# Long convolution woven between weight units in a two-layer diffusion block, and slabs of modulation weights moved

## What is computed

```python
def centred_long_conv(z, h):
    zf = jnp.fft.rfft(z.astype(jnp.float32), n=n_fft, axis=1)
    hf = jnp.fft.rfft(h, n=n_fft, axis=0)
    y = jnp.fft.irfft(zf * hf[None], n=n_fft, axis=1)[:, n_tok // 2:n_tok // 2 + n_tok]
def hyena_mixer(h, w_in, b_in, conv_w, conv_b, filt, skip, w_out, b_out):
    u = centred_short_conv(h @ w_in + b_in, conv_w, conv_b)
    x1, x2, v = jnp.split(u, HYENA_ORDER + 1, axis=-1)
    z = x1 * (centred_long_conv(v, filt[:, 0]) + v * skip[0])
    z = x2 * (centred_long_conv(z, filt[:, 1]) + z * skip[1])
    return z @ w_out + b_out
...
        x = x + g1 * y_lat
        x = x + g2 * sq_relu_mlp(modulate(rms_norm(x, norm_mlp_g[i]), sh2, sc2), mlp_w1[i], mlp_w2[i])
```

## Time and profile before

| | |
|---|---|
| median of 3 runs | 2640.75 us (2637.38 to 2641.97) |
| the profiled execution's own time | 2644.23 us |
| its span | 2642.4 us |
| TensorE busy | 2471.6 us (94%) |
| VectorE busy | 1955.2 us (74%) |
| ScalarE busy | 1167.6 us (44%) |
| mean granted TensorE clock | 0.964 |
| DMA | 610.10 MB, mean 231 GB/s |

### The profile page before, as it was taken

One profiled execution on the slowest core, in us unless ns is written; L12 is line 12 of the kernel. 1 busy time (PEld: TensorE's weight loads), 2 busy tenths in 40 slices (PEclk: granted clock), 3 DMA queues, 4 the chain that ended last, 5 costly groups with the idle time before them and its releaser, 6 DMA issues.

```text
span 2642.4 us, 40626 instructions
## 1 busy us (share of the span) xinstructions
PE 2471.6 (94%) x13316; PEld 2077.0 (79%) x13316; DVE 1955.2 (74%) x2322; ACT 1167.6 (44%) x1595; POOL 0.2 (0%) x4
## 2 busy tenths in 40 slices
PE   6879989798999999999989899899899999999998
PEld 2248867587888888888878778787788888888887
DVE  6767777687987878878878888888765565565665
ACT  2334256435344444444454325234544444444444
POOL 0000000000000000000000000000000000000000
PEclk9989998898999999999989999999899999999998
DMA  8857865576988888888777658576665565665653
GB/s 306 319 183 247 277 194 171 168 269 234 351 299 279 281 279 280 269 283 280 263 241 243 211 195 278 173 247 213 201 190 187 187 190 186 187 190 185 189 189 121
DMA packets 441193, 610.10 MB, mean 231 GB/s; under 512 B 18875, under 2 KB 383644, under 8 KB 439068
## 3 DMA queue, kind: packets, MB, share of 16 engines
q1 hardware_dynamic: 439676, 599.98, 68.4%
q10 hardware_dynamic: 1440, 9.18, 1.0%
HBM read 596.50 MB, written 10.49 MB: 230 GB/s over the span
## 4 chain that ended last, share of the span: by engine, by line
PE 71%; DVE 13%; issue 6%; ACT 6%; DMA 3%; SPq 0%; DVEq 0%; ACTq 0%
PE ps L359 42%; PE ps L368 22%; DVE acc L456 2%; DVE w_lo L444 2%; PE ps L1100 2%; ACT w_hi L440 2%; DMA raw<-in_mlp_w 1%; ACT hm L875 1%; DVE sm L1751 1%; DMA raw<-in_attn_w_out 1%; PE ps L1136 1%; PE ps L1117 1%; DVE u L646 1%; PE ps L1326 1%; ACT probs L1465 1%
## 5 line engine op out<-in xcount | busy, mean ns | idle before, releaser
L444 DVE TENSOR_TENSOR w_lo<-raw,w_hi 128x1024 fp32r<-128x1024 f32 x720 | 877.3, 1224 | 495.5 <-ACT w_hi L440 491.7
L440 ACT ACTIVATE w_hi<-raw 128x1024 fp32r<-128x1024 f32 x720 | 758.9, 1059 | 1030.5 <-PE ps L368 813.6
L359 PE MATMUL ps<-lat,w_hi 128*128 128x512 f32 x3136 | 816.2, 400 | 31.0 <-DVE lat L864 18.3
L359 PEld LDWEIGHTS ps<-lat,w_hi 128*128 128x128 f32 x3136 | 575.9, 192 | 140.1 <-issue 24.5
L359 PE MATMUL ps<-alt,w_hi 128*128 128x512 f32 x2624 | 674.4, 396 | 11.2 <-DVE alt L1738 5.9
L359 PEld LDWEIGHTS ps<-alt,w_hi 128*128 128x128 f32 x2624 | 476.3, 190 | 97.9 <-issue 6.7
L368 PEld LDWEIGHTS ps<-lat,w_lo 128*128 128x128 f32 x3136 | 435.3, 192 | 31.4 <-DVE w_lo L444 0.4
L368 PE MATMUL ps<-lat,w_lo 128*128 128x256 f32 x3136 | 447.6, 284 | 0.0
L456 DVE SCALAR_TENSOR_TENSOR acc<-slab,silu,acc 128x1024 f32<-128x1024 f32 x300 | 380.2, 1280 | 8.9 <-DMA slab<-in_mod_w 6.8
L368 PEld LDWEIGHTS ps<-alt,w_lo 128*128 128x128 f32 x2624 | 363.7, 192 | 26.4 <-DVE w_lo L444 0.6
L368 PE MATMUL ps<-alt,w_lo 128*128 128x256 f32 x2624 | 374.4, 283 | 0.2 <-DVE w_lo L444 0.2
(11 more groups left out here) (191 smaller groups left out, 1512.4 us busy)
## 6 DMA issues: line engine op xcount, KB each, us to landing
raw<-in_mlp_w SPq DMA_DIRECT2D x512, 512.0 KB, 3.7
slab<-in_mod_w SPq DMA_DIRECT2D x352, 512.0 KB, 5.9
raw<-in_hy_w_in SPq DMA_DIRECT2D x96, 512.0 KB, 6.6
raw<-in_attn_w_in SPq DMA_DIRECT2D x48, 512.0 KB, 4.6
raw<-in_mod_w SPq DMA_DIRECT2D x32, 512.0 KB, 6.7
raw<-in_attn_w_out SPq DMA_DIRECT2D x32, 512.0 KB, 4.9
raw<-in_hy_w_out SPq DMA_DIRECT2D x32, 512.0 KB, 7.0
spec_dram<-spec ACTq DMA_DIRECT2D x8, 1024.0 KB, 6.9
```

What stands on the lines that cost most here:

```text
L359: e.matmul(ps[:, bank, :], w_hi[:, n % RING, kk, fb * P:(fb + 1) * P], t[:, kb, :], start=(kb == 0), stop=False)
L440: e.activation(w_hi[:, n % RING], raw[:, n % RING], ACT.Copy).then_inc(hi_ready, 1)
L444: e.tensor_tensor(w_lo[:, n % RING], raw[:, n % RING], w_hi[:, n % RING].bitcast(F32), ALU.subtract).then_inc(split_ready, 1)
```

## The change

The chunk loop is unrolled in all engines, and each step of the long convolution is given a place by number: t counts units from the chunk's first, 24 to a chunk, and steps with t of 24 or more stand between units of the next chunk. For the last chunk they stand in the first call of the output projection, whose units take another order so that the ones that need the last chunk's z come last, and whose readout (`FirstOut`) starts behind the seventh unit. PSUM banks 4 to 7 serve the convolution, u of v becomes double-buffered (u0), and skip is part of multiply. The hyena keeps eight slabs a chunk, in two of its three calls (halves 8 and 9, both closed by one `pe_close`); half 7 comes with the output projection, halves 10 and 11 with the second MLP's first four up calls, eight slabs a call, finished behind them.

```diff
-        SL_HOUT = Slabs(1, [11], 4, M_HOUT)
+            return Slabs(1, [8 + c // 2], 4, M_HY + 2 * c, 8 * (c % 2), c // 2)
+        HOUT_ORDER = ((0, 0), (0, 1), (0, 2), (1, 0), (1, 1), (1, 2), (0, 3), (1, 3))
+        SL_HOUT = Slabs(1, [7], 4, M_HOUT)
+        SL_UP1 = Slabs(1, [10, 11], 8, M_UP1)
+        def at_conv(places, c, k, n):
+            for (t, hf), what in places.items():
+                for chunk in (c - 1, c):
+                    if 0 <= chunk < 4 and t == 24 * (c - chunk) + 8 * k + n:
+                        yield what, chunk, hf
...
+            for c in range(4):
+                    sp_iter(e, T_HY + 3 * c + k, a["hy_w_in"], 0, (c + part * 4) * 512, k, sl_hy(c) if k < 2 else None,
+                            {(0, 4): 2 * c - 1, (1, 1): 0 if c == 0 else None, (2, 1): 2 * c if c else None}, k)
...
+            CONV_PE = {(14, 0): "turn0", (15, 1): "turn0", (18, 0): "spectrum0", (19, 1): "spectrum0",
+                       (23, 0): "invert0", (24, 1): "invert0", (28, 0): "turn1", (29, 1): "turn1",
+                       (32, 0): "spectrum1", (33, 1): "spectrum1", (37, 0): "invert1", (38, 1): "invert1"}
...
-                pe_finish(e, M_HY + 4 * c + 4, FIN_HY + c, 1)
+            for n in range(8):
+                g, j = HOUT_ORDER[n]
+                if n == 0:
+                    invert(3, 0, 1)
+                if n in (2, 3):
+                    turn(3, 1, n - 2)
+                if n in (4, 5):
+                    spectrum(3, 1, n - 4)
+                if n == 6:
+                    invert(3, 1, 0)
+                    invert(3, 1, 1)
+                    pe_close(e, M_HOUT, FIN_HY, 7)
+                pe_unit(e, T_HOUT, n, g, j, alt, (z_ready, 8 if j == 3 else 6))
...
+            CONV_ACT = {(17, 0): "copy0", (18, 1): "copy0", (31, 0): "copy1", (32, 1): "copy1", (42, 0): "round", (43, 1): "round"}
...
+            CONV_DVE = {(13, 0): "fold0", (13, 1): "fold0", (21, 0): "multiply0", (22, 1): "multiply0",
+                        (26, 0): "combine0", (27, 1): "combine0", (35, 0): "multiply1", (36, 1): "multiply1",
+                        (40, 0): "combine1", (41, 1): "combine1", (43, 0): "rest", (44, 1): "rest"}
...
+            for n in range(8):
+                dve_split(e, T_HOUT, n)
+                if n in (1, 2):
+                    combine(3, 0, n - 1)
+                    fold(3, 1, n - 1)
+                if n in (4, 5):
+                    multiply(3, 1, n - 4)
+                if n == 6:
+                    combine(3, 1, 0)
+                    combine(3, 1, 1)
+                    round_rest(3, 0)
+                    round_rest(3, 1)
+                    dve_close(e, FIN_HY, [mod_col(1, 8), mod_col(1, 9)], 7)
+            dve_slabs(e, SL_HOUT, 0, 0, 4)
+            first_h.dve_head(e, T_HOUT, 0)
...
             def gains_mlp1():
-                e.wait_ge(mod_ready, FIN_HOUT + 1)
+                dve_finish(e, FIN_HOUT, [mod_col(1, 7)])
...
-            mlp(1, 0, None, None, None, None, None)
+            mlp(1, 0, None, SL_UP1, None, None, (FIN_UP1, [mod_col(1, 10), mod_col(1, 11)]))
```

More of the change, by code:

```diff
@@ L1374, in _, with turn @@
-            pe_call(e, T_HOUT, 4, alt, lambda i: lambda j: (z_ready, 8), 4)
-            pe_enter(e, 4, 9, lambda: pe_finish(e, M_END, FIN_HOUT, 1))
-            with e.Fori(0, w_ff - 1) as q_:
+            def turn(c, o, hf):
+                e.wait_ge(folded[hf], 2 * c + o + 1)
+                for tb in range(2):
+                    for fb in range(2):
+                        mm = e.transpose(ps[:, 5 + 2 * hf, tb * 256 + fb * P:tb * 256 + (fb + 1) * P],
+                                         z_tok[:, hf, tb, fb * P:(fb + 1) * P], ident)
+                mm.then_inc(turned, 1)
@@ new lines, in spectrum @@
+            def spectrum(c, o, hf):
+                if c == 0 and o == 0:
+                    e.wait_ge(in_fwd, 16)
+                    e.wait_ge(mod_ready, FIN_HY + 1)
+                e.wait_ge(tok_ready, 2 * (2 * c + o) + hf + 1)
+                if o == 0:
+                    e.wait_ge(conv_v[hf], 6 * c + 1)
+                for f in range(4):
+                    mm = e.matmul(ps[:, 4 + 2 * hf + f // 2, (f % 2) * 256:(f % 2 + 1) * 256],
+                                  fwd[:, f * P:(f + 1) * P], z_tok[:, hf, SIDE[f], :], start=True, stop=True)
+                mm.then_inc(z_spec, 1)
@@ new lines, in invert @@
+            def invert(c, o, hf):
+                if c == 0 and o == 0:
+                    e.wait_ge(in_back, 16)
+                e.wait_ge(spec_v, 6 * (2 * (2 * c + o) + hf) + 6 + 6)
+                for fb in range(2):
+                    for f in range(4):
+                        mm = e.matmul(ps[:, 4 + 2 * hf, fb * TOK:(fb + 1) * TOK],
+                                      y_spec[:, hf, f, fb * P:(fb + 1) * P], back[:, f, :],
+                                      start=(f == 0), stop=(f == 3))
+                mm.then_inc(y_back, 1)
@@ L1377, in _ @@
+            with e.Fori(1, 4) as i:
+                pe_iter(e, T_HOUT + i, alt, lambda j: (z_ready, 8), None, (4, i - 1))
+            pe_enter(e, 4, 9, lambda: pe_finish(e, M_UP1, FIN_HOUT, 1))
+            mlp_q(1, 0, None, True)
+            with e.Fori(1, w_ff - 1) as q_:
                 mlp_q(1, q_)
@@ new lines, in round_rest, with conv_dve @@
+            def round_rest(c, hf):
+                e.wait_ge(z_hi, 2 * c + hf + 1)
+                e.tensor_tensor(alt[:, ds(4 * c + 2 * hf, 2), TOK:2 * TOK], u0[:, c % 2, 2 * hf:2 * hf + 2],
+                                alt[:, ds(4 * c + 2 * hf, 2), 0:TOK].bitcast(F32),
+                                ALU.subtract).then_inc(z_ready, 1)
+            def conv_dve(what, c, hf):
+                if what == "fold0":
+                    fold(c, 0, hf)
+                if what == "multiply0":
+                    multiply(c, 0, hf)
+                if what == "combine0":
+                    combine(c, 0, hf)
+                    fold(c, 1, hf)
+                if what == "multiply1":
+                    multiply(c, 1, hf)
+                if what == "combine1":
+                    combine(c, 1, hf)
+                if what == "rest":
+                    round_rest(c, hf)
```

333 lines of the change are left out of this document (149 added, 184 removed).

## The result

| | before | after |
|---|---|---|
| median | 2641.03 us (4 runs, 2637.38 to 2641.97) | 2600.96 us (4 runs, 2599.54 to 2602.76) |
| ratio | | 0.9845, 95% interval 0.9833 to 0.9858 |
| the profiled execution's own time, span | 2644.23, 2642.4 us | 2601.12, 2598.4 us |
| instructions | 40626 | 39537 |

The forecast of 2600 holds, against the profiled execution's own time too (2603.4 said, 2601.12 measured). In the changed kernel L359, L368, L440, L444 and L456 of before are L369, L378, L450, L454 and L466; turn, spectrum and inverse are L1332, L1346 and L1356; the close is L440.

The account below looks back on a forecast made before the run. TensorE was taken as the bound (71% of the last chain), idle at hyena seams. Hyena stretch -52.6, last chunk +0.5, moved slabs +11.1, entry +0.2 sum to -40.8: 2603.4 us profiled, 2600 median; forecast 2594 to 2607, ends 2590 and 2620.

Parts of the forecast that it names:

- Seams: Hyena chunks: conv steps packed between units bring a chunk from 104.92 to 90 us, removing 14.1 us of idle and half-clock time.
- Can VectorE follow: Hyena chunks: VectorE needs 79 of 90 us, so splits stay ahead of PE; priced at nothing, at most 5 us a chunk.
- Rival 1: Hyena: splits starve, VectorE's queue or weight ring is late, PE waits 2 to 5 us a chunk; 2614 us, chance 0.15.
- Last chunk in the output projection: Output projection's first call: 0.5 us for tight steps, 3.4 for the close, 2.5 for the readout wait.
- Rival 3: Gain only in three seams, the last chunk's order in the output projection staying bare, 14 us back: 2614 us, chance 0.05.
- Slabs in the second MLP: Second MLP's first up call: 32 slabs moved there cost 11.1 us, bounds 8 and 14, as in the first MLP.
- Rival 2: Second MLP: slabs cost 4 to 8 us less than in the first MLP; 2594 us, chance 0.07.
- Entry: Second MLP's entry: one modulation half's reduction moves before the norm's statistics, costing 0 to 0.5 us, taken as 0.2.
- "Nothing ... chunks unrolled": Hyena loops: unrolling changes nothing, since chunk 0 took 104.97 us and chunk 1 104.92.
- Rival 5: Hyena seams: unrolling saves a backward-branch cost, one load's 6.6 us at three seams; 2580 us, chance 0.02.

Follow-up runs that it names:

- loads alone: Changed kernel, all 32 slabs of the second MLP loaded but VectorE multiplying only 32 of 1024 columns of each: 2598.31 us.
- adds alone: Changed kernel, the second MLP's 32 slabs not loaded, VectorE adding stale slots at full length: 2591.72 us.
- the other series: Changed kernel, unaltered, run again beside the variants with 12 and 16 slabs a chunk: median 2603.02 us, ratio 0.985 to before.

## Why the prediction was right

**Seams (right).** Chunks 90 forecast, 89.8 by its own terms (24 x 2.793 + 22.8), 89.59 measured, PE without a pause. The price of a step when packed between units carried over: a spectrum 1.54 (1433.81 to 1435.35) and the unit behind it 0.19 longer together make the 1.73 taken from the earlier trace rows. The inverse was taken as 3.5 from bare records; woven it is 3.26 plus 0.20 for the longer unit (1544.09 to 1547.08, less 2.79), 3.46; four of them explain 0.16 of the 0.24 us a chunk by which these terms were too high. A turn is 0.36 (1561.71 to 1562.07) plus 0.09 for the longer unit, 0.45 and not 0.47, and four of them explain the other 0.08.

**Can VectorE follow (right, with a wrong reason beside it).** 79 us forecast, 78.2 to 79.5 measured. But the argument made the lower load look needed; 87.44 us of 89.60 did as well. The place in the queue decided, not the busy share: two units of room for the multiply, none left at three, 2.2 us a chunk then. Rival 1 (splits starve) did not occur in a chunk of 16 slabs either.

**Last chunk in the output projection (right, with a slow unit unforeseen).** Forecast 0.5 + 3.4 + 2.5 = 6.4. Measured: close 3.49, no wait for z, a slow unit behind the close that nobody foresaw (3.45 us to its second part where 1.84 is usual, 1.6 more), a wait of 1.04 for the readout: 6.1. The slow unit and the wait share one stretch of 11.9 us, so they are not two costs but one, set by VectorE's readout. Where the unit was quick (loads alone, adds alone) the wait was 2.59 us, the forecast's 2.5. That the close covers the wait for z, as the step had said, the kernel without it shows: 3.24 us of waiting stand in its place, and S falls by 0.6. Rival 3 did not occur.

**Slabs in the second MLP (right).** 11.1 forecast from the first MLP, 10.0 measured in the profiled execution, 8.5 to 11.9 in the five other woven kernels' executions with the same MLP (114.52 without the close, 116.94 with the close split, 117.49 to 118.00 for the changed kernel in the other series and the two with multiplies later, less 106.06); eight units take 24.17 us, 24.3 forecast. The runs show DMA as the cause, as the step had said. Rival 2 (4 to 8 less) did not occur.

**Entry (right).** 0.2 forecast, 0.13 measured.

**"Nothing ... chunks unrolled" (wrong, without harm).** The step compared chunk 0 with chunk 1 and found 104.97 and 104.92. But chunk 0 carries 2.9 us of start-up, which the same text states, and is outside the loop on ScalarE and VectorE. The totals were equal because chunk 1 had a slow first unit (3.62 for 2.09) and a seam 1.2 us longer (34.69 against 33.50), although chunk 0's seam held a slow spectrum too; against the same seam unrolled it was 2.9 us longer. Unrolling alone gives 10.5 us of S and 7.1 us of time in one run. The sum was unharmed, because it priced the new stretch from its parts and not the old one less its idle time; only the credit is split otherwise, about 10 us for unrolling and about 39 (515.51 to 476.62) for the weave. The Trainium skill (Runtime: NRT & Kernel Launch, Instruction fetch mechanics) has runtime control flow as expensive through the fetch at a taken branch; the trace agrees that a loop costs, but shows the cost in hand-overs within the pass, 1.42 against 1.16 us, and none at the branch. Rival 5's 20 us did not occur; 2.9 to 3.3 us a looped seam did, of which the pauses are shown to come from the loop and the slow spectra are not.

**Against the median.** -40.8 forecast, -44.0 between spans, -40.07 between medians: the profiled execution of before lay 3.2 us above its median, that of after 0.2 above.

## What to carry to other kernels

Work that stands bare between two streams of matmuls costs its pauses, and the low clock around them, on top of its instructions, here 14.1 us a chunk beside the 22.8 of all conv steps; priced by its start-to-start time in a packed place, its woven cost can be forecast to 1%. Before moving load off an engine that looks nearly full, ask whether the queue's order or its sum is short: VectorE at 98% did no harm here, and a layout with 12 slabs a chunk was 11.5 us faster than the change, while the slabs moved away met a stretch where DMA was the limit. And two passes are a comparison only when they are the same code: a first pass with a start-up, peeled on some engines, hid what the loop cost.

## What the hardware showed that I had not expected

- A loop lengthens waits where nothing of the loop itself is seen: 1.42 instead of 1.16 us from ScalarE to VectorE, twice a seam, because a register instruction ahead of the activation and one ahead of the taps take the wait and then 0.15 and 0.11 us.
- VectorE can be busy for 22.28 of 22.35 us, and PE, which needs its output for each unit, waits for nothing in that stretch.
- Two units with the same instructions before them ran at different levels of the clock in different executions (hi part 2.09 or 3.6 us behind the close), a pause of 3.24 us was followed by a unit of 2.08, one of 2.59 by one of 3.63, and a spectrum behind pauses of 1.90 and 0.69 us took 3.66 in one seam and, behind 1.88 and 0.69, 1.99 in another.
